# A fused decoder layer on one core: HGRN decay levels joined in fours, squares summed in two fp32r parts, and the work around them reordered

## The reference, cut to what matters

```python
att = jnp.einsum('bhtd,bhsd,bhtsd->bhts', qq, kk, jnp.exp(rel))   # rel = A[t] - A[s], s <= t
o_intra = jnp.einsum('bhts,bhse->bhte', att, vv)
...
o_c = rms_norm(o_c, hgrn_norm[l].reshape(HG_HEADS, HG_VDIM)).reshape(B, T, C_WIDTH) * jax.nn.silu(c_silu)
```

## Time and profile before

| | us |
|---|---|
| median of 3 runs | 486.56 (486.48 to 486.65) |
| the profiled execution | 485.57 |
| its span | 483.8 |
| PE busy in the span | 475.2 (98%) |
| DVE busy | 343.2 (71%) |
| ACT busy | 264.6 (55%) |
| POOL busy | 159.1 (33%) |

### The profile page before, as it was taken

How to read it: one execution, slowest core, us unless ns; L and a number is a source line. 1 busy time by engine, 2 the same in 40 slices (tenths; PEclk the granted TensorE clock), 3 DMA queues, 4 the chain that set the end, 5 groups by cost and what they waited for, 6 DMA issues and landing times.

```text
span 483.8 us, 9621 instructions
## 1 busy us (share of the span) xinstructions
PE 475.2 (98%) x3948; PEld 463.9 (96%) x3948; DVE 343.2 (71%) x577; ACT 264.6 (55%) x398; POOL 159.1 (33%) x157
## 2 busy tenths in 40 slices
PE   9999999999999999899999999999999999999995
PEld 8999999999999999889999999999999999999995
DVE  4898967798976566797896747878584257655653
ACT  6887744594562737553565346576554245433531
POOL 1074820807100009990256415436745120000000
PEclk9999999999999999999999999999999999999999
DMA  8956634454354755555355343253525536677502
GB/s 297 330 170 192 189 103 143 125 171 142 119 175 122 188 137 166 155 164 184 119 187 162 106 133 113 87 156 107 174 89 173 175 120 192 213 233 246 175 1 87
DMA packets 76006, 76.43 MB, mean 158 GB/s; under 512 B 5759, under 2 KB 74751, under 8 KB 75963
## 3 DMA queue, kind: packets, MB, share of 16 engines
q1 hardware_dynamic: 75675, 75.64, 50.4%
q10 hardware_dynamic: 288, 0.18, 0.2%
HBM read 74.77 MB, written 1.05 MB: 157 GB/s over the span
## 4 chain that ended last, share of the span: by engine, by line
PE 94%; DVE 2%; ACT 2%; issue 1%; DVEq 0%; ACTq 0%
PE ps L997 75%; PE ps L1022 4%; PE ps L1160 3%; PE ps L1111 2%; PE ps L1185 1%; PE ps L1100 1%; PE ps L1179 1%; PE ps L1127 1%; DVE WL L629 1%; PE ps L1023 1%; PE ps L1114 1%; PE ps L1038 1%; PE ps L1129 1%; PE ps L1128 1%; PE ps L1065 1%
## 5 line engine op out<-in xcount | busy, mean ns | idle before, releaser
L997 PE MATMUL ps<-hH,WL 128*128 128x256 f32 x688 | 195.6, 288 | 1.2 <-DVE WL L629 1.2
L997 PE MATMUL ps<-hL,WH 128*128 128x256 f32 x688 | 194.8, 284 | 0.0
L997 PE MATMUL ps<-hH,WH 128*128 128x256 f32 x688 | 194.8, 284 | 0.0
L629 DVE TENSOR_TENSOR WL<-W,WH 128x2048 fp32r<-128x2048 f32 (+1 forms) x66 | 152.9, 2317 | 19.5 <-PE ps L997 17.1
L432 ACT ACTIVATE WH<-W 128x2048 fp32r<-128x2048 f32 (+1 forms) x66 | 124.7, 1889 | 47.9 <-PE ps L997 46.6
L997 PEld LDWEIGHTS ps<-hH,WL 128*128 128x128 f32 x688 | 130.6, 191 | 2.3 <-DVE WL L629 1.4
L997 PEld LDWEIGHTS ps<-hL,WH 128*128 128x128 f32 x688 | 131.8, 192 | 0.8 <-issue 0.7
L997 PEld LDWEIGHTS ps<-hH,WH 128*128 128x128 f32 x688 | 131.7, 191 | 0.0
L394 POOL TENSOR_SCALAR R<-R,st 128x256 f32<-128x256 f32 x32 | 29.2, 924 | 82.1 <-DVE st L804 82.1
L997 PE MATMUL ps<-bH,WL 128*128 128x256 f32 x192 | 54.9, 286 | 0.0
L997 PE MATMUL ps<-bH,WH 128*128 128x256 f32 x192 | 54.3, 283 | 0.0
(11 more groups left out here) (192 smaller groups left out, 779.3 us busy)
## 6 DMA issues: line engine op xcount, KB each, us to landing
W<-w_in SPq DMA_DIRECT2D x48, 1024.0 KB, 5.2
W<-w_branch SPq DMA_DIRECT2D x12, 1024.0 KB, 5.3
W<-w_out SPq DMA_DIRECT2D x4, 1024.0 KB, 5.4
W<-w_in SPq DMA_DIRECT2D x2, 608.0 KB, 3.8
R<-x SPq DMA_DIRECT2D x2, 512.0 KB, 4.6
W<-w_in SPq DMA_DIRECT2D x2, 512.0 KB, 6.7
R<-cmp_w SPq DMA_DIRECT2D x2, 512.0 KB, 8.5
OC<-pool_w SPq DMA_DIRECT2D x4, 256.0 KB, 5.9
```

Source lines behind the costliest of these rows:

```text
L629: dve.tensor_tensor(slab_view(WL[:, s % 2], s), slab_view(W[:, s % 3], s), slab_view(WH[:, s % 3], s), ALU.subtract).then_inc(s_lo, 1)
L997: mm = pe.matmul(o, l, r, start=(at == 0 if mixed else k0 + k == 0 and j == 0), stop=(at == len(order) - 1 if mixed else k0 + k == KC - 1 ...
```

## The change

- **Levels.** Instead of the levels 128, 64, 32, 16, 8, 4 there is a top (128), a half (64), and two joined levels with blocks of 16 and of 4. In a joined level a key's factor runs to the end of its own block (`OWN`, 256 columns for each head), a query's factor to the edges of the up to three blocks before it in its group of four (`REACH`, 384 columns for each head). A unit's scores are two fp32 matmuls of 192 columns, one of 64, one of 128, and in every second unit another of 128.
- **POOL** does for each pair two operations of 256 columns (as before, for 64), for each joined level one of 512 (`OWN`) and three of 384, 256 and 128 (`REACH`), and the two of 512. For pair 1 it also waits for the first head's multiplication.
- **ACT's exponential** covers 4096 columns for each pair instead of 3584.
- **DVE** has six masked copies for the joined levels (of 96, 64 and 32 columns, twice) and one plain copy of 64 partitions x 64 columns instead of the five for levels, and nine multiplications for each head instead of seven. These stand ahead of `lo` now, in a function `multiply`, at slabs 7, 10, 11, 14, 15, 18, 19, 22. Scans are at slabs 2, 5, 6, 8.
- **Squares.** ACT writes them once in fp32 and once rounded to fp32r (`SQH`), DVE makes the difference (`SQL`, 512 columns, at slabs 13, 17, 21, 25), PE sums both with fp32r ones: two matmuls of 512 columns, at slabs 15, 19, 22, 26.
- **Order of slabs.** `kc`, `vc` at 12, 13, then `q` 2, `vs`, `vwk` and `vw` (16, 17), `bv` 0 and 1, `q` 0 and 1, `bv` 2 and 3, `ks` (24), `kw` (25), `q` 3 (26). For `ks` and `kw` DVE does the next `lo` ahead of reading them.
- **kc and vc** are copied by ACT; the positions are put through the same matmul as a 61st column and row.
- **Start.** The identity and the small parameters are loaded by SP ahead of slab 0, not by ACT. Half of x's second tile is squared on DVE and half scaled on ACT. `WH` and `WL` of the first half of slab 0 are made in two pieces.
- **End.** DVE adds the first three sums ahead of time, so that the root takes the last sum and the rest as its bias.

```diff
-LEVELS = (128, 64, 32, 16, 8, 4)
+RADIX = (16, 4)
+STEPS = ((0, 3, 1), (3, 2, 2), (5, 1, 3))
...
-SCAN_AT = (2, 6, 10, 14)
+SCAN_AT = (2, 5, 6, 8)
+MUL_AT = (7, 10, 11, 14, 15, 18, 19, 22)
+RSTD_AT = (15, 19, 22, 26)
+NORM_AT = (16, 20, 23, 27)
...
+SQL_AT = tuple(U0 + 4 + 4 * p for p in range(HG // 2))
...
             for p in range(4):
                 pool.wait_ge(s_scan, p + 1)
+                if p == 1:
+                    pool.wait_ge(s_hmul, 1)
...
+                for r, b in enumerate(RADIX):
+                    n = 2 * T // b
+                    av = a2.rearrange("p (n w) -> p n w", w=b)
+                    pool.tensor_tensor(OWN[p % 2][r].rearrange("p h (n w) -> p (h n) w", w=b),
+                                       k2.rearrange("p (n w) -> p n w", w=b),
+                                       av[:, :, b - 1:b].to_broadcast((P, n, b)), ALU.add)
+                    aw = a2.rearrange("p (n j w) -> p n j w", j=4, w=b)
+                    to = REACH[p % 2][r].rearrange("p h (n j w) -> p (h n) j w", j=6, w=b)
+                    for at, count, far in STEPS:
+                        pool.tensor_tensor(to[:, :, at:at + count], aw[:, :, far:4],
+                                           aw[:, :, 0:count, b - 1:b].to_broadcast((P, n // 4, count, b)), ALU.subtract)
...
+                        if h >= 2:
+                            act.wait_ge(s_hss, h // 2)
+                        act.activation(SQH[:, h % 2], ps[:, 6, 0:T], ACT.Square).then_inc(s_sqh, 1)
...
+            def multiply(s):
+                for h in range(HG):
+                    if s == MUL_AT[h]:
+                        dve.wait_ge(s_hexp, h // 2 + 1)
+                        dve.wait_ge(s_read_a, ACT_READS[WHERE[("hq", h // 2)]])
...
+                        for r, b in enumerate(RADIX):
...
+                            for at, count, far in STEPS:
+                                dve.tensor_tensor(ev[:, :, at:at + count], ev[:, :, at:at + count], qv[:, :, far:4],
+                                                  ALU.mult)
...
+                        dve.tensor_tensor(SQL.rearrange("p e t -> p (e t)"), SQ.rearrange("p e t -> p (e t)"),
+                                          SQH.rearrange("p e t -> p (e t)"), ALU.subtract).then_inc(s_sql, 1)
...
                 early(s)
-                if mixing(s - 1):
+                multiply(s)
+                if mixing(s - 1) and SLABS[s][0] != "kw":
                     lo(s + 1)
                 mix(s)
+                keys = SLABS[s][0] in ("ks", "kw")
+                if keys:
+                    lo(s + 2)
                 read(s)
...
-                for lv in range(1, NLV):
...
-                    pe.matmul(ps[:, b0, 64 * (lv - 1):64 * lv], t, up, start=(lv == 1), stop=False)
...
+                for r in range(2):
+                    pe.matmul(ps[:, b0, 192 * r:192 * r + 192], OWN[e][r][:, hp, t],
+                              REACH[e][r][:, hp, 192 * i:192 * i + 192], start=(r == 0), stop=False)
+                pe.matmul(ps[:, b0, 384:448], HALF[e][:, hp, t], HALF[e][:, hp, P * i + 64:P * i + P],
+                          start=False, stop=True)
...
-                        pe.matmul(ps[:, 7, :], ones, SQ.rearrange("p e t -> p (e t)"), start=True,
+                        pe.matmul(ps[:, 7, :], ONE[:], SQH.rearrange("p e t -> p (e t)"), start=True, stop=False)
+                        pe.matmul(ps[:, 7, :], ONE[:], SQL.rearrange("p e t -> p (e t)"), start=False,
                                   stop=True).then_inc(s_hss, 1)
...
-            for i in range(TT):
-                act.wait_ge(s_x[i], 16)
-                link(act.activation(sq[:, i, :], xin[:, i, :], ACT.Square, accum_out=st_x[:, i:i + 1]))
...
+            act.activation(WH[:, 0, 0:2, :], W[:, 0, 0:2, :], ACT.Copy).then_inc(s_hi0a, 1)
+            act.wait_ge(s_small, 16)
             for c in range(KC):
+                if c == 2:
+                    act.activation(WH[:, 0, 2:FIRST_A, :], W[:, 0, 2:FIRST_A, :], ACT.Copy).then_inc(s_hi0a, 1)
```

More of the change, by code:

```diff
@@ L131, in trunk @@
         PM = sb("PM", [P, 2, 640])
+        with nc.sbuf_tensor("SQH", [P, 2, T], F32R) as SQH:
+            pass
         PT1 = sb("PT1", [P, 768])
         CP = sb("CP", [P, 2048])
+        with nc.sbuf_tensor("rho_place", [P, 512], F32), nc.sbuf_tensor("SQL", [P, 2, T], F32R) as SQL:
+            pass
         BR = sb("BR", [P, 2, 512])
@@ L470, in mix @@
                 if s == CK:
-                    act.wait_ge(s_cpe, 2)
+                    act.wait_ge(s_ckf, 1)
                     for half in range(2):
-                        last = act.activation(CKS[64 * half:64 * half + 64, 0, :, 0:NCMP], ck_out, ACT.Copy)
+                        last = act.activation(CKS[64 * half:64 * half + 64, 0, :, 0:NCMP], CKF, ACT.Copy)
                     last.then_inc(s_ckh, 1)
@@ L543, in read @@
                                    ACT.Sigmoid).then_inc(s_read_a, 1)
+                elif kind in ("kc", "vc"):
+                    v = 0 if kind == "kc" else 1
+                    for r in range(2):
+                        win = b2[:, :, CS * r:CS * r + CS * NCMP].rearrange("p q (c j k) -> p k q c j", j=CS // 2, k=2)
+                        to = XB[:, v, 8 * r:8 * r + 8, 0:CROWS - 1].rearrange("p j (q e c) -> p e q c j", q=2, e=2)
+                        for e in range(2):
+                            for k in range(2):
+                                last = act.activation(to[64 * k:64 * k + 64, e], win[64 * e:64 * e + 64, k], ACT.Copy)
+                    last.then_inc(s_read_a, 1)
                 elif kind == "bv":
@@ L922, in _ @@
                     merged_lo(3)
-                if s + 2 < NS and not mixing(s):
+                if s + 2 < NS and not mixing(s) and not keys:
                     lo(s + 2)
@@ L1044, in compress @@
                 pe.wait_ge(s_cw, 32)
-                pe.wait_ge(s_read_v, DVE_READS[WHERE[("vc", 0)]])
+                pe.wait_ge(s_read_a, ACT_READS[WHERE[("vc", 0)]])
+                pe.wait_ge(s_pos, 1)
                 pe.wait_ge(s_hoc, HG)
                 for j in range(CB // 2):
-                    keys, values = (cpe[:, a, j].rearrange("p g c -> p (g c)") for a in range(2))
+                    keys, values = (XB[:, a, j] for a in range(2))
                     end = dict(start=(j == 0), stop=(j == CB // 2 - 1))
-                    mk = pe.matmul(ck_out.rearrange("p g c -> p (g c)"), WC[:, 0, j, :], keys, **end)
-                    mv = pe.matmul(ps[0:GROUPS * NCMP, 6, 0:HEAD], values, WC[:, 1, j, :], **end)
+                    mk = pe.matmul(ck_all, WC[:, 0, j, :], keys, **end)
+                    mv = pe.matmul(ps[0:CROWS, 6, 0:HEAD], values, WC[:, 1, j, :], **end)
                 mk.then_inc(s_cpe, 1)
@@ L1172, in first_product @@
                         pe.wait_ge(s_hx, TT + k + 1)
[L1173 removed]
+                        if k < FIRST_A:
+                            pe.wait_ge(s_hi0a, k // 2 + 1)
+                        else:
+                            pe.wait_ge(s_hi0b, 1)
                     elif w is WH:
```

270 lines of the change are left out of this document (152 added, 118 removed).

## The result

The changed kernel takes 491.51 us (487.12 to 494.07, 19 runs) against 486.46 us (485.14 to 486.85, 19 runs): ratio 1.0112, 95% interval 1.0094 to 1.0129. It is 1.1% slower. The forecast was 480.8 with a range of 478.8 to 484.4. The profiled execution is the longest of the 19, 494.07 us with a span of 492.2, against 485.57 and 483.8 before.

A forecast was written before the change was run, and what follows sets the result against it. PE's own work was taken as the bound. Terms -3.2 - 1.6 - 1.8 - 0.2 + 0.4 + 0.4 + 0.2 = -5.8 took 485.57 to 479.8 us, a median of 480.8; range 478.8 to 484.4.

The forecast's parts named there:

- Scores: HGRN units' score matmuls on PE: 1.14 us a unit against 1.34, -3.2 us over 16 units (bounds -6.5 and +0.2).
- Squares: Four sums of squares on PE: two fp32r matmuls at 0.47 replace one fp32 at 0.86, -1.6 us.
- Cover at slabs 9 to 24: Slabs 9 to 24: operations added on DVE and ACT run beside PE and cost it +0.2 us (0 to +4).
- at slabs 14 and 15, hardly before: Where a read of q is added, lo would end hardly before PE wants it; elsewhere about 1 us before.
- a wait for `WL` at slab 16: Sign of a wrong forecast: PE waiting for WL at slabs 15, 16, 19 or 20, through POOL or DVE's load.
- Stalls at 202 and 209: PE's two waits, 2.2 us in all, could go whole through DVE's new order: -1.8 us (bounds -2.7 and 0).
- `lo` of slabs 28 to 31: DVE's low parts named as late next, with ACT waiting at 27 for DVE's sum; covered by the -1.8 term's bounds.
- the gain at 202 to 209 comes back: Rival, chance 0.10: -1.8 becomes 0 and the start takes its +1.2, giving 483.4 us.
- Start and slabs 1 to 8: Two terms: DVE's later start +0.4 us (-0.2 to +1.2), and lo of slab 6 late +0.4 (0 to +1.2).
- End: End of the kernel: DVE's addition, 0.17 us with its hand-over, leaves the chain, -0.2 us.
- POOL: the rival: Rival, chance 0.06: POOL's joined levels take 24 us in pair 3 against 16 available, giving 490.8 us.
- the 1.0 us that the forecast adds between profile and median: Median run of 486.56 us against profiled execution's 485.57, so the result 479.8 was moved up to 480.8.

The follow-up runs named there:

- e1_copies: The changed kernel with ACT copying kc and vc with the inner loop over the 15 blocks instead of the 8 steps: 489.11 us, ratio 1.0073.
- e3_start: The changed kernel with the start of the kernel before (identity by ACT's queue, x normalised as before, WH and WL in one piece): 489.61 us.
- e6_unmix: The changed kernel with the 32 small compressed-score matmuls ahead of slab 31's product instead of mixed into it: 490.23 us, ratio 1.0081.
- e9_order: The changed kernel with kc/vc copies reordered, lo(29) and lo(31) ahead of reading slabs 27 and 29, PC clearing and gates at slab 31: 480.07 us.
- e10_all: e9_order with the start of the kernel before and DVE's small copies of positions and ONE at slab 12: 479.95 us, ratio 0.9879.
- e13_pool: e9_order with one more wait of POOL, holding its pair 0 work until lo(5) is made: 480.46 us, ratio 0.9891.
- e2_lo29: The changed kernel with DVE making lo of slabs 29, 30 and 31 ahead of its slab's other work: 492.40 us, ratio 1.0041.
- e5_cx30: The changed kernel with DVE's clearing of PC, gates and CVD operations at slab 30 instead of 29: 495.07 us, ratio 1.0172.
- e12_wait: e9_order with two clearings put on DVE behind lo(31), ahead of reading slab 29, to make PE wait: 489.20 us, ratio 1.0048.

## Why the prediction was wrong

**Scores: right.** Four records of 192 columns take 0.65 us (0.162 each, the value that the line between 256 and 512 gave), the 64-column pair 0.17 against 0.21 forecast. The chain of the changed kernel:

```profile
64.45 0.65 PE ps L1093 x4
65.11 0.17 PE ps L1095 x2
65.27 0.28 PE ps L1097 x2
...
138.97 0.24 PE ps L1141
139.21 0.24 PE ps L1142
```

A unit costs 1.10 against 1.34: 16 x 0.24 = -3.8, more than forecast. **Squares: nearly right**, 0.48 for a pair (forecast 0.47). From one product to the next a square took 0.85 before, 0.79 in front of the half slab, so the three in slabs 9 to 24 give 1.1 against 1.2. The fourth, in slabs 25 to 28, takes 0.66 now and gives 0.2 and not 0.4.

**Cover at slabs 9 to 24: one price wrong.** DVE's operations came out as priced, 0.195 to 0.270 for the masked copies, 1.29 for the six joined multiplications. ACT's copies of `kc` and `vc` were taken at 0.38, "between 0.21 and 0.6 each by its nearest forms". They take 0.626, above the upper bound, eight a slab, and the exponential of pair 2 comes 2.6 us later than in e1_copies for it. I did name the place (a read of `q` "at slabs 14 and 15, hardly before") and the sign (a wait for `WL` at slab 16), though as POOL's doing, and gave its size as 0.2 with 4 as the upper bound. PE lost 3.3 us there, a gap of 2.79 and the wider distances around it, by the traces in which the clock stayed full (e3_start, e6_unmix); 1.5 more where the clock fell too; and 0.35 ahead of slab 23. That is 5.1 in the profiled execution: all of what scores and squares gave, 3.8 and 1.1. The copies in the other order have the forecast price, 0.375, and the term is then 1.1.

**Stalls at 202 and 209: the step that failed.** This term stood at -1.8, with bounds of -2.7 and 0. Up to slab 28 it was nearly so: -1.7, with 0.2 of it a square, and -2.67 in e9_order, where the wait of 0.9 ahead of slab 29 is gone too. But the same paragraph names `lo` of slabs 28 to 31 as late next, and then bounds its cost by nothing worse than the gain given back. What happened: PE came 1.7 us sooner to slab 29 and DVE only 0.5. The wait that the paragraph names, ACT at slab 27 behind DVE's sum, held DVE up until 205.86, and from there it had no pause; so 1.56 us of the gain were waited for ahead of slab 31. And behind this wait TensorE's clock stood at half for 13.65 us, which cost 6.5 more. No term and no rival of the prediction has a price for a fall of the clock. The wait is the rival "the gain at 202 to 209 comes back"; its price was 2.6, 0.8 of it the start's, and slabs 29 to 31 alone cost 8.1. The trace of the kernel before shows no fall inside the program behind its waits of 1.2 and 1.0 us, so the earlier trace rows gave no hint of it. The times of more executions do: the kernel before has some at 484.9 to 485.6 with a clock of 0.997 to 1.0, and others at 486.4 to 486.9 with 0.995 or 0.996. The three behind the forecast's median were all of the second kind and the profiled one of the first.

**Is it the wait?** Three things were tried. Without the wait (e9_order, e10_all, e13_pool: 13 executions, 479.7 to 480.9 us, clock 0.997 to 1.0) no execution fell, and the time is near the forecast's. With a wait put back into that version 10 of 12 fell. With a wait put into the kernel before, 3 of 10 fell to the length seen in the changed kernel. The Trainium skill ("TensorE: Matmul & The Clock Gate", section HAM oscillation — how this bites in real kernels) tells of a kernel that drops to half clock at each wait for a transfer; the waits here are for DVE, shorter (1.55 to 2.8 us, the page's 3 to 5), single, and in an otherwise full PE, and the fall behind them agrees with it in kind. What decides in a single execution stays open, and so does why one kernel falls in 3 of 10 and others nearly always. The waits of the falling kernels are 1.55 to 2.8 us long, but e2_lo29 had one of 1.9 with the clock at full, and of the five traces with the same 2.79 us ahead of slab 16 the clock fell in three (the changed kernel, e2_lo29, e5_cx30) and not in two (e3_start, e6_unmix).

**Start and slabs 1 to 8.** +1.1 and +1.1 instead of +0.4 and +0.4 in this execution. The first is in part this execution's own: over the traces the changed start costs 0.7 on average (16.5 against 15.8), 0.3 above the forecast. The second is real, within its bounds, and had the wrong cause: not DVE's later start but its operations beside POOL's joined levels. **End: right**, -0.3 with what lies between.

**POOL: the rival was wrong.** Pair 3's operations ran from 117.08 to 133.3, 16 us and not 24, at the threshold that I had worked out, and no wait shows at slabs 19 or 20.

**The sum.** In the version without the two waits, e9_order, the sum is near what was measured, -5.5 on the spans against -5.8. That it is so near is partly luck, since its parts are off both ways: the scores gave 0.6 more and slabs 25 to 28, their square left out, 0.7 more; the squares gave 0.3 less, the cover cost 0.9 more and slabs 1 to 8 0.7 more; and the start came out at 0.0 instead of +0.4 in an execution that began early (16.02, against 16.5 on average). The median, 480.07, is below the 480.8 only because the 1.0 us that the forecast adds between profile and median isn't there: the profiled execution took 480.16, 0.4 above the 479.8 of the sum.

## What to carry to other kernels

A gain on the engine that bounds the time is a debt of the engines behind it: for each of them, follow the queue from the gain on and mark the first instruction that will now be late, with everything that the bounding engine waits for there (`lo`, the read of the bank, the CVD semaphore), since moving one ahead makes another late. Order a queue by when its results are wanted: work wanted late (here a clearing for slab 33) doesn't stand ahead of work wanted next. And price a short wait of TensorE by more than its length: 1.56 us ahead of a stretch with small matmuls cost 8.1 in the end, 6.5 of it by the clock.

## What the runs showed of the hardware

- Behind a PE wait of 1.55 to 2.8 us the granted clock could go to half, between 0.6 us ahead of the restart (e5_cx30, slab 16) and 2.1 us behind it (e1_copies, slab 31), and stay there: 3.4 us at slab 16 (products of 304 columns), 13.65 or 17.1 at slab 31 (256 columns with 32-column ones between), 10.2 in the one trace with the small ones in front. The same kernel on the same chip does it in some executions only.
- A wait costs PE more than the gap that the profile shows, at full clock too: 2.79 us of gap cost 3.3 (e3_start, e6_unmix, slab 16) and 3.4 (e12_wait's two executions at full clock), 0.39 cost 0.7 (e9_order).
- An ACT copy of 64 x 240 elements from PSUM took 375 or 626 ns by the order of its loops alone.
- fp32 matmuls of 192 columns cost 0.162 us a record, those of 64 columns 0.085 when there are two in a row, against 0.106 in a row of ten. All at full clock.
- A matmul of 32 columns between two of 256 adds about 0.11 us: a pair takes 0.227, a product's matmul alone 0.120.
